# One broadcast multiplication for a pair's probabilities, and nsa's output casts on VectorE

## What is computed

```python
def masked_softmax(s, mask):
    s = jnp.where(mask, s.astype(jnp.float32), -jnp.inf)
    m = jnp.max(s, axis=-1, keepdims=True)
    e = jnp.where(mask, jnp.exp(s - m), 0.0)
    d = jnp.sum(e, axis=-1, keepdims=True)
    return e / jnp.where(d > 0, d, 1.0)
...
p_win = masked_softmax(s_win, wmask)
o_win = jnp.einsum('bgrnqk,bnkgd->bnqgrd', p_win.astype(vwb.dtype), vwb)
o = (gates[:, :, 0, :, :, None] * o_cmp + gates[:, :, 1, :, :, None] * o_slc
     + gates[:, :, 2, :, :, None] * o_win).astype(h.dtype)
return o.reshape(B_, S_, NSA_HEADS * dh) @ w_out
```

## Time and profile before

| | us |
|---|---|
| three runs | 2218.06, 2218.97, 2219.67 (median 2218.97) |
| the profiled execution | 2219.71 |
| its span, first to last instruction | 2217.9 |
| PE busy in the span | 2179.4 (98%) |
| DVE busy | 1780.8 (80%) |
| ACT busy | 1161.6 (52%) |

### The profile page before, as it was taken

One profiled execution on the slowest core, in us unless ns is written; L12 is line 12 of the kernel. 1 busy time (PEld: TensorE's weight loads), 2 busy tenths in 40 slices (PEclk: granted clock), 3 DMA queues, 4 the chain that ended last, 5 costly groups with the idle time before them and its releaser, 6 DMA issues.

```text
span 2217.9 us, 37734 instructions
## 1 busy us (share of the span) xinstructions
PE 2179.4 (98%) x15156; PEld 1951.7 (88%) x15156; DVE 1780.8 (80%) x3512; ACT 1161.6 (52%) x2042; POOL 0.2 (0%) x4
## 2 busy tenths in 40 slices
PE   7999999999999999999999999999999999999998
PEld 7878889898889988996988897898888889979998
DVE  7888978689887898878898877577877876478898
ACT  4776556565553655558655645443222236376543
POOL 0000000000000000000000000000000000000000
PEclk9999999999999999999999999999999999999999
DMA  7426665466565566660666531015454523434663
GB/s 248 143 77 228 232 200 196 164 208 237 193 209 187 204 233 202 220 210 33 209 237 201 188 117 65 20 58 172 161 182 167 170 80 105 137 93 155 214 233 121
DMA packets 70014, 371.99 MB, mean 168 GB/s; under 512 B 7376, under 2 KB 16720, under 8 KB 38096
## 3 DMA queue, kind: packets, MB, share of 16 engines
q1 hardware_dynamic: 61328, 359.95, 47.9%
q10 hardware_dynamic: 8512, 9.63, 1.4%
HBM read 367.46 MB, written 1.05 MB: 166 GB/s over the span
## 4 chain that ended last, share of the span: by engine, by line
PE 88%; DVE 7%; ACT 3%; DMA 2%; issue 1%; ACTq 0%; DVEq 0%
PE ps L499 85%; DVE w_lo L2064 1%; DVE hid_f L2452 1%; DMA w_raw<-weights 1%; DVE hid_f L2474 1%; PE ps L780 1%; PE ps L843 1%; ACT hid_f L1587 1%; ACT hid_f L1597 1%; PE ps L827 0%; ACT w_hi L1387 0%; DVE X L2195 0%; PE ps L768 0%; DVE X L2342 0%; DVE a_both L2064 0%
## 5 line engine op out<-in xcount | busy, mean ns | idle before, releaser
L499 PE MATMUL ps<-a_both,w_hi 128*128 128x256 f32 (+1 forms) x4848 | 1052.8, 328 | 14.9 <-DVE a_both L2126 10.8
L499 PEld LDWEIGHTS ps<-a_both,w_hi 128*128 128x128 f32 x4848 | 805.6, 190 | 87.9 <-issue 13.0
L2064 DVE TENSOR_TENSOR w_lo<-w_raw,w_hi 128x1024 fp32r<-128x1024 f32 (+2 forms) x630 | 704.9, 1146 | 100.0 <-ACT w_hi L1387 82.2
L499 PE MATMUL ps<-a_both,w_lo 128*128 128x256 f32 (+1 forms) x3128 | 711.8, 292 | 0.0
L1387 ACT CAST w_hi<-w_raw 128x1024 fp32r<-128x1024 f32 (+2 forms) x434 | 400.0, 970 | 325.8 <-DMA w_raw<-weights 324.5
L499 PEld LDWEIGHTS ps<-a_both,w_lo 128*128 128x128 f32 x3128 | 520.1, 191 | 23.7
L499 PE MATMUL ps<-hid_both,w_hi 128*128 128x512 f32 (+2 forms) x2184 | 519.6, 348 | 1.1 <-DVE w_lo L2064 0.5
L499 PEld LDWEIGHTS ps<-hid_both,w_hi 128*128 128x128 f32 x2184 | 377.0, 190 | 53.3 <-issue 5.7
L499 PE MATMUL ps<-hid_both,w_lo 128*128 128x256 f32 (+2 forms) x1444 | 334.8, 304 | 0.0
L499 PEld LDWEIGHTS ps<-hid_both,w_lo 128*128 128x128 f32 x1444 | 234.1, 191 | 16.3
L1393 ACT CAST w_hi<-w_raw 128x1024 fp32r<-128x1024 f32 (+1 forms) x196 | 200.5, 1023 | 1.6 <-DMA w_raw<-weights 1.6
(11 more groups left out here) (239 smaller groups left out, 1899.8 us busy)
## 6 DMA issues: line engine op xcount, KB each, us to landing
w_raw<-weights SPq DMA_DIRECT2D x248, 1024.0 KB, 4.9
pe_sb<-weights SPq DMA_DIRECT2D x96, 512.0 KB, 5.7
w_raw<-weights SPq DMA_DIRECT2D x64, 704.0 KB, 4.0
pe_sb<-na_bias ACTq DMA_DIRECT2D x32, 128.0 KB, 2.2
X<-x_t SPq DMA_DIRECT2D x2, 512.0 KB, 7.2
X<-c_rows ACTq DMA_DIRECT2D x2, 512.0 KB, 4.1
qk<-qk ACTq DMA_DIRECT2D x4, 256.0 KB, 7.0
qk<-ctx_t ACTq DMA_DIRECT2D x1, 1024.0 KB, 5.7
```

The source lines that it names most:

```text
L499: return nc.tensor.matmul(out, stationary, moving, start=start, stop=stop)
L2064: return v.tensor_tensor(out, a, b.bitcast(F32), ALU.subtract)
```

## The change

The factors of a pair get one entry for each 128 columns: a new tensor `recip_blocks` of 4 x 8 values per partition, in which a factor stands twice. nsa writes it with the multiplication by the gates, moba with the reciprocal itself, whose input is broadcast. The 4 multiplications by a scalar operand become one multiplication of two tensors, 768 columns by the factors broadcast over 128 columns each. Items with one block a head (na) keep their instructions. In nsa the high part of an output tile is cast by DVE instead of ACT, at step i for item i-4, behind reduce(i) and ahead of normalize(i-1); moba keeps it on ACT.

```diff
@@ -172,6 +172,7 @@
         negmax = sb("negmax", [P, 4, 4])
         sums = sb("sums", [P, 4, 4])
         recip = sb("recip", [P, 4, 4])
+        recip_blocks = sb("recip_blocks", [P, 4, 8])
         mod_g, mod_b = sb("mod_g", [P, KD, 2]), sb("mod_b", [P, KD, 2])
         alpha_g, alpha_b = sb("alpha_g", [P, KD]), sb("alpha_b", [P, KD])
         spare = sb("spare", [P, 1])
@@ -1602,7 +1603,7 @@
                 t = ITEMS[name][b]["tile"]
                 nc.scalar.copy(a_hi[:, t, LAT], ps[:, banks[t % 2], 0:S]).then_inc(att[name]["o_hi"], 1)
 
-            def pair_attention(name, beside=None, behind=None, load_bias=None):
+            def pair_attention(name, beside=None, behind=None, load_bias=None, cast_outputs=True):
 
                 items = ITEMS[name]
                 N = len(items)
@@ -1619,7 +1620,7 @@
                     if behind:
                         behind(i)
                     b = i - 3
-                    if 0 <= b and items[b]["last"]:
+                    if cast_outputs and 0 <= b and items[b]["last"]:
                         pair_high(name, b, PAIR_O)
 
             def skip(rings, times=1):
@@ -1724,7 +1725,7 @@
                     if len(ITEMS[f"nsa{j}"]) <= i < len(ITEMS[f"nsa{j}"]) + 2:
                         split_half(late_unit + 2, i - len(ITEMS[f"nsa{j}"]))
 
-                pair_attention(f"nsa{j}", beside, behind)
+                pair_attention(f"nsa{j}", beside, behind, cast_outputs=False)
                 mixer_ends(col("norm_ffn", 3 * j * KD, KD), "A")
 
             def run_moba(_):
@@ -2461,31 +2462,53 @@
                 w = 2 * len(rows)
                 g = ITEMS[name][b]["gate"]
                 dve.wait_ge(a["exp_done"], b + 1)
-                step(v.reciprocal(recip[:, b % 4, 0:w], sums[:, b % 4, 0:w]))
-                if g is not None:
+                if len(rows) == 1:
+                    step(v.reciprocal(recip[:, b % 4, 0:w], sums[:, b % 4, 0:w]))
+                    sync()
+                    for e in range(2):
+                        at = p_pair(name, b)[:, e * W:(e + 1) * W]
+                        last = v.tensor_scalar(at, at, recip[:, b % 4, e:e + 1], None, ALU.mult)
+                    last.then_inc(a["p_ready"], 1)
+                    return
+
+                def twice(x):
+                    return x.unsqueeze(3).to_broadcast([P, 2, 2, 2])
+
+                blocks = recip_blocks[:, b % 4, :].rearrange("p (e r d) -> p e r d", e=2, r=2)
+                total = sums[:, b % 4, :].rearrange("p (e r) -> p e r", e=2)
+                if g is None:
+                    step(v.reciprocal(blocks, twice(total)))
+                else:
+                    step(v.reciprocal(recip[:, b % 4, 0:w], sums[:, b % 4, 0:w]))
                     sync()
                     both = recip[:, b % 4, :].rearrange("p (e r) -> p e r", e=2)
-                    step(v.tensor_tensor(both, both, gate[:, :, g:g + REP + 1:REP].rearrange("p r e -> p e r"), ALU.mult))
+                    step(v.tensor_tensor(blocks, twice(both), twice(gate[:, :, g:g + REP + 1:REP].rearrange("p r e -> p e r")), ALU.mult))
                 sync()
-                for e in range(2):
-                    for r, (c, _) in enumerate(rows):
-                        at = p_pair(name, b)[:, e * W + c.start:e * W + c.stop]
-                        x = len(rows) * e + r
-                        last = v.tensor_scalar(at, at, recip[:, b % 4, x:x + 1], None, ALU.mult)
-                last.then_inc(a["p_ready"], 1)
+                at = p_pair(name, b).rearrange("p (e n c) -> p e n c", e=2, c=P)
+                by = recip_blocks[:, b % 4, :].rearrange("p (e n) -> p e n", e=2)[:, :, 1:4].unsqueeze(3).to_broadcast([P, 2, 3, P])
+                v.tensor_tensor(at, at, by, ALU.mult).then_inc(a["p_ready"], 1)
+
+            def pair_high(name, b, banks):
+
+                dve.wait_ge(att[name]["pv_done"], b + 1)
+                t = ITEMS[name][b]["tile"]
+                v.tensor_copy(a_hi[:, t, LAT], ps[:, banks[t % 2], 0:S]).then_inc(att[name]["o_hi"], 1)
 
             def pair_low(name, t, banks):
 
                 dve.wait_ge(att[name]["o_hi"], t + 1)
                 minus(a_lo[:, t, LAT], ps[:, banks[t % 2], 0:S], a_hi[:, t, LAT]).then_inc(att[name]["o_ready"], 1)
 
-            def pair_attention(name, out_unit, beside=None, bias=False, begun=0):
+            def pair_attention(name, out_unit, beside=None, bias=False, begun=0, cast_outputs=False):
 
                 items = ITEMS[name]
                 N = len(items)
                 for i in range(begun, N + 4):
                     if i < N:
                         pair_reduce(name, i, PAIR_S[i % 2], bias)
+                    b = i - 4
+                    if cast_outputs and 0 <= b and items[b]["last"]:
+                        pair_high(name, b, PAIR_O)
                     if 0 <= i - 1 < N and (begun or i != 2):
                         pair_normalize(name, i - 1)
                     if i == 1 and not begun:
@@ -2701,7 +2724,7 @@
                     v.tensor_tensor(p_cmp.rearrange("p (n c) -> p n c", c=32)[:, :, 0:CS], rows3,
                                     cmp_sum[:, :].unsqueeze(2).to_broadcast([P, 2 * HEADS, CS]), ALU.mult).then_inc(s["cmp_p"], 1)
 
-                pair_attention(f"nsa{j}", u + 2, beside, begun=1)
+                pair_attention(f"nsa{j}", u + 2, beside, begun=1, cast_outputs=True)
                 mixer_ends(col("norm_ffn", 3 * j * KD, KD), "A")
 
             def run_moba(_):
```

## The result

Timed against the kernel before on one chip, 18 runs each, the changed kernel took 2221.12 us (median, 2218.77 to 2229.76) and the one before 2217.68 us (2215.34 to 2222.91). The ratio is 1.0017 with a 95% interval of 1.0010 to 1.0024: 3.8 us slower (2.2 to 5.3; the two medians alone differ by 3.4), where the sum had 3.1 us. The loss is small, under the 0.2% that the prediction called no change, but with 18 runs a side the interval leaves 1 out. Of the absolute time forecast, 2222.1 us, 1.0 was too much; in the longer series the kernel before was itself 1.3 us under the median that I started from.

A forecast was written before the change was run, and what follows sets the result against it. The prediction took a loop of DVE and PE to bound nsa. Two stages of 0.74 us in the loop plus 0.8 at the end, 3.1 us, raised 2218.97 to 2222.1 us; range 2218.5 to 2226.5.

The forecast's parts named there:

- the sum: Whole kernel: two nsa stages each lose 0.74 us in the loop and 0.8 at the end, 3.1 us together.
- What bounds the loop: nsa loop: DVE and PE together set the pace, DVE at 5.23 of 5.31 us; ACT rides along.
- ScalarE was the bound: Rival for the nsa loop: ScalarE sets the pace, the period falls to 5.05 us, time 2217.0 us; 8%.
- The multiplication: Pair normalization on DVE: one broadcast multiplication at 0.87 us replaces four taking 0.92; a pair gains 0.04 us.
- The rivals at 1.16 us and at its whole 0.95 us: Multiplication on DVE: slow broadcast at 1.16 us, 2228.0 us, 11%; dear hand-overs, 0.95 us and casts 0.45, 2225.2 us, 13%.
- The cast in the loop: nsa loop on DVE: each cast holds it 0.34 us, period 5.50 us, 0.74 us lost per stage up to pair 13.
- the cast doesn't reach the path: Rival for the nsa loop: DVE waits for PE anyway, so the cast costs nothing; 2219 to 2220 us; 6%.
- The end of the stage: Last output tiles of nsa: two casts cost DVE 0.90 us, about 0.1 covered; PE stalls 0.8 us.
- ACT's relief worth nothing, moba unchanged: ACT loses 8 casts a stage, 0.26 us each, gaining nothing; moba counts 0, at most 0.3 us gain.
- PE idle for longer than 0.61 us before every second turn: Sign of a right prediction in the nsa loop: PE's wait before every second turn exceeds 0.61 us.
- The inner bounds: Whole kernel: the bounds of cast and stage end give 2221.4 to 2223.5 us.
- the clock's dip: Second nsa stage: granted clock at 0.50 for a 1.40 us stretch, worth 0.7 us; scatter, no term of the forecast.

The follow-up runs named there:

- mult_only: The changed kernel with nsa's high-part casts back on ScalarE, only the broadcast multiplication kept; 2215.30 us, ratio 0.9996 to the kernel before.
- cast_only: The changed kernel with the four scalar multiplications back, nsa's casts still on VectorE; 2220.91 us, ratio 1.0023 to the kernel before.
- double_cast: The changed kernel with a second cast of tiles 0 to 5 into a tensor nobody reads; 2220.81 us in one run.
- tail_on_act: The changed kernel with the casts of output tiles 6 and 7 given back to ScalarE; 2217.79 us, ratio 1.0004 to the kernel before.
- cast_late: The changed kernel with VectorE's cast moved behind the normalization, directly ahead of the low part that reads it; 2222.07 us in one run.
- mult_swap: mult_only with PE's values of item i-3 ahead of the turn of item i-2; 2217.77 us, ratio 1.0004 to the kernel before.
- scores_first: mult_only with PE's values a step later, behind the next scores and ahead of the turn; 2215.31 us, ratio 0.9992 to the kernel before.

## Why the prediction was right

*What bounds the loop.* Right. DVE has no gap in the changed kernel's period, ACT has: its timeline shows the copy late by a wait for PE.

```profile
129.81 0.80 ACT L1598 COPY hid_f<-ps 128x768 f32<-128x768 f32 x1 [0.17 <-PE ps L828]
```

The rival "ScalarE was the bound" wanted a period of 5.05 us and got 5.46, and ACT's full window was a lag being worked off (mult_only).

*The multiplication.* Right, 0.88 us where I had 0.874. The rivals at 1.16 us and at its whole 0.95 us fall, and so does the loss of 0.40 us a pair that the prediction had worked out from the perf-mode table of the Trainium skill (VectorE: DVE Perf Modes, "The perf-mode tier table (the rule you actually need)"). Cast_only minus after shows a gain of 0.58 us for 14 pairs.

*The cast in the loop.* Right in kind and price (0.34, by double_cast 0.33), a little too dear in the sum. The period came out at 5.46 us instead of 5.50: a step without a tile is 109.97 - 107.57 = 2.40 instead of 2.41, one with a cast and a low part 113.03 - 109.97 = 3.06 instead of 3.09. So turn(15) came 0.64 us later than before, the stage having begun 0.06 later: 0.58 us lost in the loop, 0.74 forecast. By the periods it is 5 x 0.15 for the steps with a tile, less 4 x 0.04 for the pairs before them, 0.59; averaged over four periods the growth is 0.14 us, which makes it 0.54. The rival that the cast doesn't reach the path falls with cast_only and double_cast.

*The end of the stage.* Right. From DVE's first weight half to the last low part it took 141.95 - 139.34 = 2.61 us, now 143.51 - 139.99 = 3.52: 0.91, forecast 0.90. PE used 0.06 us of cover where I took 0.1. From turn(15) to the last tile PE needs 143.99 - 137.58 = 6.41 us, 0.86 more than the 142.49 - 136.94 before; I had 0.8. The bracket shows 0.68 us of it.

*ACT's relief worth nothing, moba unchanged.* Right, by the windows. That handing casts back to ACT shortens the stage (tail_on_act, mult_only) is the same finding from the other side.

*The sum.* Per stage 0.58 + 0.86 = 1.44 from PE's rows, 1.50 by the memset; two stages 2.9 to 3.0 us, forecast 3.1, timed 3.8 (2.2 to 5.3). That the sum fits so well has some luck in it: the loop was 0.16 us a stage too dear and the end 0.06 too cheap, and the two partly cancel. The inner bounds were also added up a little wide: with the terms given they are 2221.6 and 2223.2 us, not 2221.4 and 2223.5.

*Two things were wrong.* Under "what would show it" I wanted PE idle for longer than 0.61 us before every second turn; it was 0.48. The step that failed is which turn the cast delays: its pair is turned in the other half of the period, where the wait has no bracket (0.98 against 0.76 us from scores to turn). And I priced the clock's dip at 0.7 us, from the 1.40 us stretch that the earlier trace rows show. That stretch was a part of it: the stage with the dip took 56.23 us, one without 54.65, so it cost 1.58 us.

## What to carry to other kernels

Where two engines look full, don't ask which is fuller: add up each engine's start-to-start distances over a period late in the loop, and the chain that runs through two engines, and set them beside the measured period. ACT was the fullest and for a while started each operation the moment the last one let it, only because it was behind. Work taken from an engine below the period is worth nothing, and work given to the one that fills it costs its start-to-start distance. This distance depends on the successor: 0.34 us for a cast followed by something that doesn't read it, 0.45 directly ahead of its reader; so look also at the end of a stage, where two casts cost more (0.86 us) than five in the loop (0.58 us net of the multiplication's gain). Before moving work between engines, look at the order on the third: here moving PE's values away from between turn and scores gave 0.48 us a stage on top of the multiplication's 0.38. And when one chain is cut, the next is close: the loop went from 5.27 us to 5.16, and there ScalarE stopped it.

## What the runs showed of the hardware

**A dip of the clock that comes and goes.** Windows of the kernel before, of the changed kernel and of cast_only, in which the eighth number is the granted clock:

```profile
997.60:1001.00 3.40, 3.40 (x19) 3.40 (x19) 3.21 (x13) 2.13 (x5) 0.00 (x0) 0.54 0.60 251
```

```profile
997.60:1001.00 3.40, 3.40 (x32) 3.20 (x32) 3.09 (x4) 3.35 (x6) 0.00 (x0) 1.00 0.65 198
```

```profile
86.40:89.80 3.40, 3.40 (x19) 3.40 (x18) 2.41 (x11) 3.37 (x4) 0.00 (x0) 0.54 0.33 137
```

At three places, at about 86 us (cast_only, cast_late), 998 (before, mult_swap, scores_first) and 2020 of the span (before and others), PE ran at the lower of its two levels (0.50 in the earlier trace rows, 1.2 GHz) for about 3.4 us in some executions and at the full 2.4 GHz in others. At the first two PE was busy throughout, and in the 3.6 us ahead of the dip at 998 too, at the full clock. At 86 us cast_only has run the same instructions as the kernel before, whose clock was full there. One such dip lengthened a stage by 56.23 - 54.65 = 1.58 us before and by 58.28 - 56.73 = 1.55 us in cast_only, as much as the whole change costs a stage. In scores_first it lasted some 10 us at 997, and that execution took 2219.57 us against its median of 2215.31. This is a part of the scatter of the run times: of the 21 runs of the kernel before beside scores_first, the three with a mean granted clock of 0.995 or 0.996 took 2221.33 to 2222.02 us, the eight at 0.998 took 2215.70 to 2218.09. It is why spans can't be compared here and stages can. The Trainium skill (TensorE: Matmul & The Clock Gate, "What's actually happening") has the activity windows run free of the kernel's start; dips that come or stay away at one place fit that, though no run here separates it from other causes.

**Broadcast is free.** Factors broadcast over 128 columns cost 4 ns on 954. The Trainium skill (VectorE: DVE Perf Modes, "The TRN2 errata — SBUF-src ops pay a fixed extra latency per instruction") gives (N + 151) / 0.96 ns for a float32 addition of two tensors of N columns; for 768 that is 957, and the broadcast multiplication measured 958.
